# Shifting the activation tiles by half of 128 bytes against the weight tiles in SBUF

## The chip, the cores and the metric

The kernel runs on one core of a Trainium2 chip. The metric is the device time of one execution in microseconds: before the change the median of 3 runs is 2000.13 us (1999.19 to 2002.28).

## The reference, cut to what matters

Four blocks of a transformer-like model follow each other on one sequence of 256 positions with 2048 features, all in float32: an MLA attention layer (16 heads), a sliding-window attention layer (32 query heads, 4 key heads), a layer that holds MoBA attention (8 heads) beside a Mamba-2 mixer, and a feed-forward layer with a causal convolution of 3 taps.

```python
h = rmsnorm(x, layer_norm[i])
y, gate = mla_mixer(...) or swa_mixer(...)         # h @ w_in, then attention
x = x + (y * silu(gate)) @ w_out                   # twice, then rmsnorm
proj = h @ w_in_2                                  # q, k, v, z, xbc, dt
mixed = concat([attn, ssm]) @ w_out_2
u = causal_depthwise_conv(rms_norm(x) @ w_ffn_up)  # 2048 x 11264
f = (gelu(gate) * up) @ w_ffn_down                 # 5632 x 2048
```

Nearly all of the arithmetic is in these products of activations (256 rows) with weights.

## The kernel before, in words

**Three products for one.** Weights come from HBM in float32. The kernel multiplies in the type fp32r, in which an operand is rounded, and gets the accuracy back by splitting both operands into a rounded part ("high") and the rest ("low"): high x high + high x low + low x high are three matmuls into the same PSUM bank.

**Weight tiles.** SyncE loads 512 KB at a time into one of four slots `raw0..raw3` (`load`, 128 partitions x 1024 float32, 4096 bytes in each partition). ScalarE rounds it into `w_high0..3` (line 1025, `split`), VectorE writes the rest into `w_low0..3` (line 1458, `split`). Each of these engines works up to three tiles (`LEAD`) ahead of TensorE. A load into a slot waits until VectorE has made the low part of the tile that was there four tiles ago; ScalarE waits until TensorE has finished with the tile four back.

**Activations.** They lie transposed, with features on the partitions: `hT_high`, `hT_low` (the normalised input of a layer, 16 chunks of 256 positions, 1024 bytes a chunk), `cT_high`, `cT_low` (the MLA layer's two low-rank inputs), `yT_high`, `yT_low` (the gated output of an attention layer) and `hidden_high`, `hidden_low` (pieces of the feed-forward layer's hidden rows).

**Two kinds of product.** `block_b` (lines 450 to 452) loads 128 columns of a weight tile into the array and streams 256 columns of activations past it. `block_a` (lines 459 to 461) loads 128 columns of activations and streams 256 or 512 columns of weights past them; `down_step` (lines 1001 to 1003) does the same for the last layer with `hidden`. In a profile of this kernel the names behind `<-` don't say which of the two is streamed: at lines 450 to 452 it is the activations, at the others the weights. Each of these matmuls needs a weight load (LDWEIGHTS) of its own. Other products (attention scores, transposes, rotations) are in plain float32, at lines 486 and 489.

**Order of the work.** Each engine's stream is written out by hand, with semaphores between them. In the attention layers TensorE's stream alternates between projections and the attention of the group of heads before, so that the softmax on VectorE and ScalarE lies under matmuls.

**Where tensors lie.** `sb(name, shape)` places a tensor in SBUF behind the one that was asked for before it, in every partition at the same address, at the next multiple of 32 bytes. An `ExitStack` that is closed gives its room back, and the next tensor takes it. The first tensor of the program, `raw0`, starts at a multiple of 128 bytes. `raw`, `w_high`, `w_low`, `x`, `nx`, `hT_high` and `hT_low` are all multiples of 128 bytes long, so each of them starts at a multiple of 128. Counting the lengths on from there gives, as the remainder of the start address by 128:

| tensors | before | after the change |
|---|---|---|
| `raw`, `w_high`, `w_low` | 0 | 0 |
| `x`, `nx`, `hT_high`, `hT_low`, `constants` | 0 | 64 |
| `gain_rows`, `small` | 0 | 64 |
| `yT_high`, `yT_low`, `hidden_high`, `hidden_low` | 32 | 64 |
| `cT_high`, `cT_low`, `q_nope`, `k_nope` and others of the group `a1` | 96 | 64 |

All slices that the split products take start a multiple of 512 bytes into their tensor, so the table holds for every one of their operands.

Of the kernel before, what the change touches and what calls it, by code (L numbers as in the profile page):

```python
# [24 lines left out]
F32 = mybir.dt.float32  # L25
# [6 lines left out]
P = 128  # L32
# [144 lines left out]
def program(nc, a, out, toeplitz):  # L177
# [3 lines left out]
    def sb(name, shape, dt=F32, where=None):  # L181
        return (where or persistent).enter_context(nc.sbuf_tensor(name, shape, dt))
# [4 lines left out]
    with ctx:  # L187
        raw = [sb(f"raw{s}", [P, TILE]) for s in range(SLOTS)]
        whi = [sb(f"w_high{s}", [P, TILE], F32R) for s in range(SLOTS)]
        wlo = [sb(f"w_low{s}", [P, TILE], F32R) for s in range(SLOTS)]  # L190
        x = sb("x", [P, TT, D])
        nx = sb("nx", [P, TT, D])
        hTh = sb("hT_high", [P, DC, SEQ], F32R)
# [13 lines left out]
        xst = gbc[:, :].rearrange("p (t n) -> p t n", t=TT)  # L207
        small = sb("small", [P, 64])
        sq = sb("group_squares", [P, TT, 4])

        att = ExitStack()
        yTh = sb("yT_high", [P, DC, SEQ], F32R, att)
# [11 lines left out]
        rc = sb("row_rcp", [P, 2, 2], F32, att)  # L224

        a1 = ExitStack()
        cosm = sb("cos_mla", [P, SEQ], F32, a1)
        sinm = sb("sin_mla", [P, SEQ], F32, a1)
        coss = sb("cos_swa", [P, SEQ], F32, a1)
# [1962 lines left out]
```

How the kernel before makes its waits and increments, by code:

```python
def wait(eng, sem, count):  # L144
    if isinstance(count, int) and count <= 0:
        return
    eng.wait_ge(sem, count)
# [2 lines left out]
def after(eng, sem, count):  # L151
    eng.wait_ge(sem, count + 1)
# [15 lines left out]
    def done(self, ins):  # L169
        ins.then_inc(self.sem, 1)
        self.off += 1
        at = self.base + self.off
        self.eng.wait_ge(self.sem, at if not self.loop else at + self.i * self.loop)
# [190 lines left out]
        @block.sync  # L365
# [1 line left out]
            def load(tile, source, shape=(2, 512), i=0, n=0):  # L367
                s = tile % SLOTS
                if tile >= SLOTS:
                    sp.wait_ge(low_made, tile - SLOTS + 1 + i * n)
                c, w = shape
                sp.dma_start(raw[s][:, 0:c * w].rearrange("p (c n) -> p c n", c=c), source).then_inc(raw_loaded[s], 16)
# [50 lines left out]
            with sp.Fori(0, FC // 4) as i:  # L424
                for j in range(8):
                    load(T_DOWN + j, rows_of[:, bass.ds(i, 1), j % 4, j // 4, :], (1, TILE), i, 8)
            for b in (0, 1, 5, 2, 3, 6, 4, 7):
                mine = BY_POOL if b in BY_POOL else BY_DVE
                sp.wait_ge(ff["fin_pool" if b in BY_POOL else "fin"], mine.index(b) + 1)
                t, g = b // 4, b % 4
                sp.dma_start(out[t * P:(t + 1) * P, g * 512:(g + 1) * 512],
                             x[:, t, g * 512:(g + 1) * 512]).then_inc(stored, 16)
            sp.wait_ge(stored, 8 * 16)
# [7 lines left out]
            def ready(tile, i=0, n=0):  # L442
                pe.wait_ge(low_made, tile + 1 + i * n)
```

## Time and profile before

| | |
|---|---|
| median of the runs | 2000.13 us |
| the profiled execution | 2002.27 us |
| its span, first to last instruction | 2000.1 us |
| TensorE busy | 1907.7 us, 95% of the span, 13112 matmuls |
| TensorE weight loads busy | 1771.1 us, 89% |
| VectorE, ScalarE, GpSimd busy | 1110.5 us (56%), 896.9 us (45%), 151.3 us (8%) |
| mean granted TensorE clock | 0.982 of 2.4 GHz |
| read from HBM | 321.14 MB |

The profile lists one execution. A matmul's duration in it (`mean ns of one`) is longer than the time that it takes the array, because a matmul's way through the array overlaps with the next one's; what counts in a stream of matmuls is the distance from one start to the next.

### The profile page before, as it was taken

The numbers are of one execution on the slowest core, as the hardware profiler recorded it, in microseconds if no ns is written. First come the engines' busy times: TensorE is split into PE (matmuls) and PEld (weight loads), VectorE is DVE, ScalarE is ACT, GpSimd is POOL, SyncE is SP. The second block draws the span as 40 slices with busy tenths as digits, with TensorE's granted clock in tenths as the row PEclk, the third lists the DMA queues.
The fourth block names the chain that finished last, engine by engine and source line by source line (L and its number), as shares of the span: only waits on it lengthen the run. The fifth ranks groups of instructions, "written<-read, shape, count | busy, mean of one in ns | idle before, by whom it ended". The sixth has DMA issues, their size and how long they took to land.

```text
span 2000.1 us, 35228 instructions
## 1 busy us (share of the span) xinstructions
PE 1907.7 (95%) x13112; PEld 1771.1 (89%) x13112; DVE 1110.5 (56%) x1575; ACT 896.9 (45%) x1347; POOL 151.3 (8%) x177
## 2 busy tenths in 40 slices
PE   6899999889999997999999997999999999999997
PEld 5799998789999875999999786999999999988885
DVE  6555565545565655665555555556555556544444
ACT  5454444444444444454344444454444444433333
POOL 1001110000011000000000000100000000023322
PEclk9899999999999998999999998999999999999999
DMA  6455545535444454455554453555556555555553
GB/s 215 144 149 144 154 153 168 168 116 160 146 132 131 127 161 143 127 161 170 157 156 144 163 189 122 183 181 185 181 180 186 179 182 185 180 184 185 187 188 115
DMA packets 234781, 324.11 MB, mean 162 GB/s; under 512 B 12272, under 2 KB 170116, under 8 KB 234080
## 3 DMA queue, kind: packets, MB, share of 16 engines
q1 hardware_dynamic: 233296, 317.63, 51.0%
q0 software_dynamic: 1136, 4.58, 0.7%
q10 hardware_dynamic: 288, 1.09, 0.2%
q8 instruction: 39, 0.64, 0.1%
q14 instruction: 22, 0.18, 0.0%
HBM read 321.14 MB, written 2.11 MB: 162 GB/s over the span
## 4 chain that ended last, share of the span: by engine, by line
PE 92%; DVE 3%; ACT 2%; issue 1%; DMA 1%; POOL 0%; ACTq 0%; DVEq 0%; SPq 0%
PE bank L450 17%; PE bank L451 17%; PE bank L452 17%; PE bank L459 7%; PE bank L461 7%; PE bank L460 7%; PE bank L486 4%; PE bank L1002 3%; PE bank L1001 3%; PE bank L1003 3%; PE scores L486 3%; PE scores L1002 1%; PE scores L1001 1%; PE scores L1003 1%; PE bank L489 1%
## 5 line engine op out<-in xcount | busy, mean ns | idle before, releaser
L1458 DVE TENSOR_TENSOR w_low<-raw,w_high 128x1024 fp32r<-128x1024 f32 x603 | 739.3, 1229 | 756.2 <-ACT w_high L1025 755.7
L1025 ACT CAST w_high<-raw 128x1024 fp32r<-128x1024 f32 x603 | 630.2, 1048 | 828.9 <-PE bank L452 467.5
L450 PE MATMUL bank<-hT_high,w_high 128*128 128x256 f32 x2672 | 765.4, 286 | 8.8 <-issue 3.1
L451 PE MATMUL bank<-hT_low,w_high 128*128 128x256 f32 x2672 | 758.4, 284 | 0.0
L452 PE MATMUL bank<-hT_high,w_low 128*128 128x256 f32 x2672 | 758.4, 284 | 0.0
L450 PEld LDWEIGHTS bank<-hT_high,w_high 128*128 128x128 f32 x2672 | 515.4, 193 | 11.8 <-issue 11.4
L451 PEld LDWEIGHTS bank<-hT_low,w_high 128*128 128x128 f32 x2672 | 515.4, 193 | 1.1 <-issue 1.0
L452 PEld LDWEIGHTS bank<-hT_high,w_low 128*128 128x128 f32 x2672 | 515.2, 193 | 0.0
L459 PE MATMUL bank<-w_high,yT_high 128*128 128x512 f32 x384 | 152.9, 398 | 1.9 <-POOL yT_low L2076 1.9
L461 PE MATMUL bank<-w_high,yT_low 128*128 128x512 f32 x384 | 152.4, 397 | 0.0
L460 PE MATMUL bank<-w_low,yT_high 128*128 128x512 f32 x384 | 151.1, 394 | 0.0
L459 PE MATMUL bank<-w_high,hT_high 128*128 128x256 f32 (+1 forms) x352 | 107.6, 306 | 0.0
L460 PE MATMUL bank<-w_low,hT_high 128*128 128x256 f32 (+1 forms) x352 | 106.4, 302 | 0.0
L461 PE MATMUL bank<-w_high,hT_low 128*128 128x256 f32 (+1 forms) x352 | 106.3, 302 | 0.0
L1001 PE MATMUL bank<-w_high,hidden_high 128*128 128x512 f32 x264 | 104.1, 394 | 1.3 <-DVE up_conv L1994 1.3
L1002 PE MATMUL bank<-w_low,hidden_high 128*128 128x512 f32 x264 | 105.3, 399 | 0.0
L1003 PE MATMUL bank<-w_high,hidden_low 128*128 128x512 f32 x264 | 103.5, 392 | 0.0
L459 PEld LDWEIGHTS bank<-w_high,yT_high 128*128 128x128 f32 x384 | 72.1, 188 | 18.8 <-POOL yT_low L2076 1.6
L461 PEld LDWEIGHTS bank<-w_high,yT_low 128*128 128x128 f32 x384 | 72.1, 188 | 17.5
L460 PEld LDWEIGHTS bank<-w_low,yT_high 128*128 128x128 f32 x384 | 72.1, 188 | 17.4
L459 PEld LDWEIGHTS bank<-w_high,hT_high 128*128 128x128 f32 x352 | 67.2, 191 | 8.5 <-issue 6.1
L461 PEld LDWEIGHTS bank<-w_high,hT_low 128*128 128x128 f32 x352 | 67.2, 191 | 2.5
(270 smaller groups left out, 2022.6 us busy)
## 6 DMA issues: line engine op xcount, KB each, us to landing
raw<-in_w_up SPq DMA_DIRECT2D x176, 512.0 KB, 4.5
raw<-in_w_in SPq DMA_DIRECT2D x88, 512.0 KB, 3.5
raw<-in_w_down SPq DMA_DIRECT2D x88, 512.0 KB, 3.5
raw<-in_w_swa SPq DMA_DIRECT2D x72, 512.0 KB, 3.5
raw<-in_w_c SPq DMA_DIRECT2D x50, 512.0 KB, 3.8
raw<-in_w_mlao SPq DMA_DIRECT2D x32, 512.0 KB, 3.8
raw<-in_w_swao SPq DMA_DIRECT2D x32, 512.0 KB, 4.1
raw<-in_w_out SPq DMA_DIRECT2D x32, 512.0 KB, 3.6
```

The lines of the kernel that those rows point to most:

```text
L450: nc.tensor.matmul(to, h, act_h[:, chunk, :], start=first, stop=False, skip_group_check=True)
L451: nc.tensor.matmul(to, h, act_l[:, chunk, :], start=False, stop=False, skip_group_check=True)
L452: return nc.tensor.matmul(to, l, act_h[:, chunk, :], start=False, stop=last, skip_group_check=True)
L459: nc.tensor.matmul(to, ah, h, start=first, stop=False, skip_group_check=True)
L460: nc.tensor.matmul(to, ah, l, start=False, stop=False, skip_group_check=True)
L461: return nc.tensor.matmul(to, al, h, start=False, stop=last, skip_group_check=True)
L486: return nc.tensor.matmul(to, lhsT, rhs, start=start, stop=stop, skip_group_check=True)
L1001: nc.tensor.matmul(to, ah, whi[s][:, w], start=first, stop=False, skip_group_check=True)
L1002: nc.tensor.matmul(to, ah, wlo[s][:, w], start=False, stop=False, skip_group_check=True)
L1003: last = nc.tensor.matmul(to, al, whi[s][:, w], start=False, stop=True, skip_group_check=True)
L1025: nc.scalar.copy(whi[s][:, :], raw[s][:, :]).then_inc(high_made, 1)
L1458: v.tensor_tensor(wlo[s][:, :], raw[s][:, :], whi[s][:, :].bitcast(F32), ALU.subtract).then_inc(low_made, 1)
```

## The change

Three tensors that nothing reads or writes are put between the others. Their lengths are 64, 96 and 64 bytes in each partition.

```diff
         wlo = [sb(f"w_low{s}", [P, TILE], F32R) for s in range(SLOTS)]
+        sb("half_a_line_x", [P, 16])
         x = sb("x", [P, TT, D])
...
         sq = sb("group_squares", [P, TT, 4])
+        sb("half_a_line_y", [P, 24])
 
         att = ExitStack()
         yTh = sb("yT_high", [P, DC, SEQ], F32R, att)
...
         a1 = ExitStack()
+        sb("half_a_line_c", [P, 16], F32, a1)
         cosm = sb("cos_mla", [P, SEQ], F32, a1)
```

No instruction is added, removed or reordered; what changes is the start address of every tensor behind the first of the three, as in the table above.

## Rows read from the trace of the kernel before

**Rows 1.** The page, chain that ended last: shares of the span by engine.
```profile
PE 92%; DVE 3%; ACT 2%; issue 1%; DMA 1%; POOL 0%; ACTq 0%; DVEq 0%; SPq 0%
```
**Rows 2.** Windows: from:to, length, busy us (x instructions) by engine, TensorE clock, DMA share, GB/s.
```profile
0.00:25.00 25.00, 7.41 (x39) 6.95 (x40) 8.70 (x22) 15.07 (x24) 6.60 (x18) 1.00 0.76 263
25.00:75.00 50.00, 49.47 (x242) 41.74 (x240) 31.53 (x48) 24.27 (x36) 1.20 (x2) 1.00 0.58 171
1280.00:1730.00 450.00, 450.00 (x3752) 450.00 (x3752) 265.28 (x335) 209.04 (x252) 6.78 (x6) 1.00 0.59 182
```
**Rows 3.** TensorE's waits: who, total us, times, longest us.
```profile
PE bank L489 <- DVE prob L1507: 5.1, 5, 1.8
```
**Rows 4.** TensorE's groups by shape, first line of each three: name, shapes, count, busy us, mean ns.
```profile
L451 PE MATMUL bank<-hT_low,w_high 128*128 128x256 f32 x2672 | 758.4, 284 | 0.0
...
L459 PE MATMUL bank<-w_high,yT_high 128*128 128x512 f32 x384 | 152.9, 398 | 1.9 <-POOL yT_low L2076 1.9
...
L1001 PE MATMUL bank<-w_high,hidden_high 128*128 128x512 f32 x264 | 104.1, 394 | 1.3 <-DVE up_conv L1994 1.3
...
L459 PE MATMUL bank<-w_high,hT_high 128*128 128x256 f32 x288 | 82.6, 287 | 0.0
...
L450 PE MATMUL bank<-cT_high,w_high 128*128 128x256 f32 x160 | 46.0, 287 | 1.8 <-DVE cT_low L1473 1.8
...
L1001 PE MATMUL scores<-w_high,hidden_high 128*128 128x512 f32 x88 | 34.7, 394 | 0.0
...
L459 PE MATMUL bank<-w_high,hT_high 128*128 128x512 f32 x64 | 25.0, 391 | 0.0
...
L459 PE MATMUL bank<-w_high,cT_high 128*128 128x256 f32 x64 | 17.9, 280 | 0.0
```
**Rows 5.** Timeline, TensorE, feed-forward up: start us, duration us; first and seventh of seven.
```profile
1399.83 0.28 PE L450 MATMUL bank<-hT_high,w_high 128*128 128x256 f32 x1
...
1400.55 0.28 PE L450 MATMUL bank<-hT_high,w_high 128*128 128x256 f32 x1
```
**Rows 6.** The same view, first projection of the MLA layer; first and seventh of seven.
```profile
59.72 0.39 PE L459 MATMUL bank<-w_high,hT_high 128*128 128x512 f32 x1
...
61.08 0.39 PE L459 MATMUL bank<-w_high,hT_high 128*128 128x512 f32 x1
```
**Rows 7.** The same view, MLA output projection; first and seventh of seven.
```profile
299.69 0.39 PE L460 MATMUL bank<-w_low,yT_high 128*128 128x512 f32 x1
...
301.09 0.39 PE L460 MATMUL bank<-w_low,yT_high 128*128 128x512 f32 x1
```
**Rows 8.** The same view, feed-forward down; first and seventh of seven.
```profile
1799.78 0.39 PE L1003 MATMUL bank<-w_high,hidden_low 128*128 128x512 f32 x1
...
1801.18 0.39 PE L1003 MATMUL bank<-w_high,hidden_low 128*128 128x512 f32 x1
```
**Rows 9.** The same view, MLA projections from cT: 1st and 12th streamed; 1st loaded, 7th behind.
```profile
249.64 0.28 PE L451 MATMUL bank<-cT_low,w_high 128*128 128x256 f32 x1
...
250.96 0.28 PE L459 MATMUL bank<-w_high,cT_high 128*128 128x256 f32 x1
...
253.81 0.28 PE L459 MATMUL bank<-w_high,cT_high 128*128 128x256 f32 x1
...
254.51 0.28 PE L450 MATMUL bank<-cT_high,w_high 128*128 128x256 f32 x1
```
**Rows 10.** Groups of TensorE's weight loads: name, shapes, count, busy us, mean ns.
```profile
L451 PEld LDWEIGHTS bank<-hT_low,w_high 128*128 128x128 f32 x2672 | 515.4, 193 | 1.1 <-issue 1.0
...
L459 PEld LDWEIGHTS bank<-w_high,yT_high 128*128 128x128 f32 x384 | 72.1, 188 | 18.8 <-POOL yT_low L2076 1.6 <-issue 0.8
```
**Rows 11.** Groups of VectorE by shape: name, shapes, count, busy us, mean ns.
```profile
L1458 DVE TENSOR_TENSOR w_low<-raw,w_high 128x1024 fp32r<-128x1024 f32 x603 | 739.3, 1229 | 756.2 <-ACT w_high L1025 755.7
...
L1473 DVE SCALAR_TENSOR_TENSOR hT_low<-scores,column_vectors,hT_high 128x256 fp32r<-128x256 f32 x16 | 6.7, 477 | 0.0
...
L1473 DVE SCALAR_TENSOR_TENSOR cT_low<-bank,column_vectors,cT_high 128x256 fp32r<-128x256 f32 x8 | 3.3, 478 | 0.0
```

## The prediction

> **What bounds the kernel now.** I read the chain of waits first: TensorE is 92% of what ended last [rows 1]. Then a window of the longest stage, the feed-forward up product: TensorE busy for all of its 450 us, at a granted clock of 1.00 (2.4 GHz), VectorE for 265 and ScalarE for 209 us [rows 2]. TensorE's waits came third: the largest within an attention stage is 5.1 us in all [rows 3]. So the time is the number of matmuls times the distance between their starts. The groups by shape give the numbers, the timeline the distances.
>
> Counts [rows 4], each row standing for three lines of equal count. Activations hT, 256 columns streamed: 3 x (2672 + 288) = 8880. hT, 512 columns: 3 x 64 = 192. yT and hidden, 512 columns: 3 x (384 + 264 + 88) = 2208. cT: 3 x 160 = 480 with cT streamed and 3 x 64 = 192 with cT loaded.
>
> Distances, each from the starts of the first and the last of a few matmuls in a row, with the remainder by 128 of the activations' address in brackets (the weights' is 0):
> - hT (0), 256 columns: (1400.55 - 1399.83)/6 = 120.0 ns [rows 5]
> - hT (0), 512 columns: (61.08 - 59.72)/6 = 226.7 ns [rows 6]
> - yT (32), 512 columns: 1.40/6 = 233.3 ns [rows 7]
> - hidden (32), 512 columns: 1.40/6 = 233.3 ns [rows 8]
> - cT (96), 256 columns, cT streamed: 1.32/11 = 120.0 ns; cT loaded: 0.70/6 = 116.7 ns [rows 9]
>
> The first two differ by 106.7 ns for 256 columns, one column per 2.4 GHz cycle. Subtracting the columns (106.7 or 213.3 ns) leaves a fixed surcharge for each matmul: hT 13.3 ns, yT and hidden 20.0 ns, cT 13.3 ns streamed and 10.0 ns loaded. The surcharge is what an address can change, since yT and hT run the same instructions and differ by 6.7 ns. In these units of 6.7 ns (16 columns, 64 bytes of float32) it is two steps at remainder 0 and three at 32. The total is 9072 x 13.3 + 2208 x 20.0 + 480 x 13.3 + 192 x 10.0 = 121.0 + 44.2 + 6.4 + 1.9 = 173.5 us, and no more than that can go.
>
> **The change part by part.** No instruction comes or goes; only addresses move.
>
> *Operands of the split products.* The remainder becomes 64 for all activations. No row shows a split product there, so bounds: the surcharge gone, 0 ns, and the largest of the rows, 20.0 ns. Which way? Two readings of the rows. First, a matmul starts together with the weight load for the next one, and both read SBUF from their first column on. With hT both begin at remainder 0, and the load itself takes 193 ns, against 188 ns where yT is loaded [rows 10]: load and stream seem to hinder each other most when both begin at the same remainder. Second, of the two places that aren't a multiple of 64, loaded activations at 32 cost 20.0 ns and at 96, 64 bytes further, 10.0 ns (there in 256 columns taken from two places): so 64 bytes against the weights are worth up to 10 ns. Applied to remainder 0, the same shift takes 13.3 to 3.3 ns. I take 6.7 ns, one step instead of two: midway between nothing left and what hT has now, since cT streamed at 96 still pays 13.3 ns. The distances become 113.3 and 220.0 ns.
>
> The terms: hT 9072 x 6.7 = 60.5 us; yT and hidden 2208 x (20.0 - 6.7) = 29.4 us; cT 480 x 6.7 + 192 x 3.3 = 3.8 us. Sum 93.7 us, all on TensorE's path.
>
> *What could give it back.* The weight tile takes 24 matmuls, 2.88 us now and 2.72 us then. VectorE's step for it is 1.23 us [rows 11], and VectorE's share in the up stage goes from 265/450 = 59% to 62%. The loads go from 182 to 193 GB/s, and 263 GB/s was moved in the first 25 us [rows 2]. Neither becomes the bound. Where TensorE already waits for the softmax (5 times, 5.1 us [rows 3]), the output products that cover the wait get shorter and the chain under them doesn't: in front of each wait stand some 24 matmuls of 512 columns, 24 x 13.3 ns = 0.3 us, so 5 x 0.3 = 1.6 us come back there; with as much again at other edges, 3 us. If that cover were not there at all, the loss would still be only the saving made under it.
>
> *The other tensors.* VectorE, ScalarE and DMA also see moved tensors. One VectorE instruction stands in the trace at two remainders, hT_low (0) 477 ns and cT_low (96) 478 ns [rows 11], so I cost these at 0; 1 ns on each of 1575 VectorE instructions would be 1.6 us of busy time, and VectorE has 44% idle. The 1112 plain float32 matmuls keep their time; bounded by the 6.7 ns that 32 bytes were worth, that is 7.4 us either way, and I keep it for the range.
>
> Sum: the profiled execution took 2002.3 us; 2002.3 - 93.7 + 3 = 1911.6 us. The median lies 2.1 us below that execution, so 1909 us.
>
> **The rivals.**
>
> *Nothing is left of the surcharge.* If both hindrances are a meeting of load and stream in the same half of 128 bytes, 64 bytes apart they never meet. I leave 2 ns. Then 9072 x 11.3 + 2208 x 18.0 + 480 x 11.3 + 192 x 8.0 = 102.5 + 39.7 + 5.4 + 1.5 = 149 us, less 5 us for waits that appear: 1856 us. For it: the 193 ns loads. Against: cT streamed, 96 away, still pays 13.3 ns, and so would hT if part of the surcharge isn't a matter of address.
>
> *Only multiples of 64 count.* Remainder 32 costs one step more than 0 because 512 bytes from there touch one 64-byte piece more; 0 and 64 are alike. Then hT stays, yT and hidden save 2208 x 6.7 = 14.7 us, cT loaded loses 192 x 3.3 = 0.6 us: 1986 us. For it: the extra 6.7 ns is just one piece. Against: cT, off the multiples as well, pays no extra.
>
> *Slower: 64 is further off than 32.* The surcharge rises with the distance from the weights: 13.3 at 0, 20.0 at 32. The place is the start of every product of lines 450 to 461, the price one more step or more, 9072 x 6.7 = 60.5 us and 480 x 6.7 + 192 x 10.0 = 5.1 us for cT, yT unchanged: 2066 us. It decides as soon as hT's surcharge rises by more than 14.7 us / 9072 = 1.6 ns, what yT may save. It would be so if the load read its columns from the last to the first: then at equal remainders load and stream begin in different halves, and 64 bytes bring them together. For it: hT to yT, the cleanest pair of rows, goes this way. Against: cT at 96 pays less than yT, and hT's loads are the long ones.
>
> *Nothing happens.* The surcharge is in the instruction and 64 bytes do nothing: 2000 us. For it: 120.0 ns both at 0 and at 96 when activations are streamed. Against: the differences of up to 10 ns among the same lines.
> The Trainium skill, "TensorE: Matmul & The Clock Gate", section "Part 2: What happens when you issue a matmul", says that TensorE has two independent SBUF read ports, so that loading the next weights takes no bandwidth from the running matmul; by that rule this case is the right one. This trace doesn't bear it out in full: 193 against 188 ns for a load, and 233.3 against 226.7 ns for a matmul. The skill's "SBUF — State Buffer", section "Door 1: The DMA port swizzle", has 16-byte cachelines, by which 0, 32, 64 and 96 would all be alike; the same two rows speak against that.
>
> **How the numbers follow.** Forecast 0.36, no surcharge left 0.18, only multiples of 64 count 0.16, nothing happens 0.08, slower 0.22. A measurement of this kernel tells a difference from about 0.2% (4 us) on. Faster are the first three, 0.70; within 0.2% 0.08 and what falls between cases, 0.09; slower 0.21. The likeliest case's own range is 1890 to 1930 us (a third of a step either way is 30 us, the float32 matmuls within it). The range that I give, 1850 to 2004 us, holds the forecast, most of the case without surcharge, the 64-byte case and no change, about 0.78; it leaves out the slower case and a surcharge of exactly 0 (2000 - 168 = 1832 us).
>
> **What would show it.** Forecast right: in the up stage 113 ns from start to start, the weight loads there at 188 ns, the output projections and the down product at 220 ns, and all counts and VectorE's 1229 ns as they are. The case of the multiples of 64: 120.0 and 226.7 ns. Slower: 126.7 ns in the up stage with loads of 193 ns or more. My number is wrong if the surcharge isn't the same in long and short products, or if hT and yT, at the same remainder then, still differ.

## The result, and the profile after

The changed kernel takes 1979.06 us (median; 1976.92 to 1981.77) against 2001.2 us for the kernel before in the same comparison: a ratio of 0.988, 95% interval 0.987 to 0.990. That is 22 us faster, where 91 us were forecast. The profiled execution's span is 1977.4 us, 22.7 us shorter than before.

First the chain that ended last, then the windows, both of the changed kernel. They answer to [rows 1] and [rows 2].
```profile
PE 91%; DVE 4%; ACT 2%; issue 1%; DMA 1%; POOL 0%; DVEq 0%; SPq 0%; ACTq 0%
```
```profile
0.00:25.00 25.00, 7.56 (x42) 6.97 (x43) 9.33 (x23) 15.32 (x25) 6.57 (x18) 1.00 0.79 270
25.00:75.00 50.00, 49.78 (x238) 41.01 (x236) 30.90 (x46) 23.64 (x34) 1.20 (x2) 1.00 0.58 168
```
TensorE still bounds the kernel. The groups by shape, which answer to [rows 4] (the matmuls are 3 lines further down in the file than before):
```profile
L454 PE MATMUL bank<-hT_low,w_high 128*128 128x256 f32 x2672 | 748.6, 280 | 0.0
...
L462 PE MATMUL bank<-w_high,yT_high 128*128 128x512 f32 x384 | 153.2, 399 | 1.9 <-POOL yT_low L2079 1.9
...
L462 PE MATMUL bank<-w_high,hT_high 128*128 128x256 f32 x288 | 81.0, 281 | 0.0
...
L462 PE MATMUL bank<-w_high,hT_high 128*128 128x512 f32 x64 | 25.4, 397 | 0.0
```
The same counts; the groups with 256 columns have become shorter, the ones with 512 have not (hT's longer, 391 to 397 ns). Weight loads of streamed hT products answer to [rows 10]:
```profile
L454 PEld LDWEIGHTS bank<-hT_low,w_high 128*128 128x128 f32 x2672 | 505.5, 189 | 1.1 <-issue 1.0
```
They fell from 193 to 189 ns. VectorE's step for a weight tile is unchanged at 1229 ns, as in [rows 11]:
```profile
L1461 DVE TENSOR_TENSOR w_low<-raw,w_high 128x1024 fp32r<-128x1024 f32 x603 | 739.1, 1229 | 737.6 <-ACT w_high L1028 737.0
```

Now the distances between starts, in the timeline of the changed kernel (start us, duration us), two rows for each form of product, six products apart. They answer to [rows 6] to [rows 8]; the last pair is loaded hT with 256 columns streamed.
```profile
59.87 0.40 PE L462 MATMUL bank<-w_high,hT_high 128*128 128x512 f32 x1
...
61.27 0.40 PE L462 MATMUL bank<-w_high,hT_high 128*128 128x512 f32 x1
...
330.02 0.40 PE L463 MATMUL bank<-w_low,yT_high 128*128 128x512 f32 x1
...
331.42 0.40 PE L463 MATMUL bank<-w_low,yT_high 128*128 128x512 f32 x1
...
1800.00 0.40 PE L1005 MATMUL bank<-w_low,hidden_high 128*128 128x512 f32 x1
...
1801.40 0.40 PE L1005 MATMUL bank<-w_low,hidden_high 128*128 128x512 f32 x1
...
919.91 0.28 PE L462 MATMUL bank<-w_high,hT_high 128*128 128x256 f32 x1
...
920.59 0.28 PE L462 MATMUL bank<-w_high,hT_high 128*128 128x256 f32 x1
```
All products with 512 columns take 1.40/6 = 233.3 ns; hT's took 226.7 ns before, so they lost. Loaded hT with 256 columns takes 0.68/6 = 113.3 ns.

For the streamed products a long window is better than six products. The rows give TensorE's busy time and in brackets its matmuls, which include one or two that were already under way when the window began. First the kernel before, then the changed one; in each the MLA output projection (loaded yT, 512 columns), then the up stage (streamed hT, 256 columns).
```profile
320.00:370.00 50.00, 50.00 (x216) 40.22 (x215) 24.63 (x24) 21.35 (x26) 2.02 (x2) 1.00 0.57 181
1300.00:1600.00 300.00, 300.00 (x2503) 300.00 (x2502) 176.01 (x221) 140.15 (x170) 1.24 (x1) 1.00 0.59 182
```
```profile
320.00:370.00 50.00, 50.00 (x216) 40.30 (x215) 25.55 (x24) 21.06 (x26) 0.00 (x0) 1.00 0.58 185
1300.00:1600.00 300.00, 300.00 (x2549) 300.00 (x2548) 179.02 (x224) 142.07 (x173) 0.00 (x0) 1.00 0.60 185
```
216 and 216 in the first window: yT gained nothing. 2503 against 2549 in the second: 300/2549 = 117.7 ns instead of 119.9. The clock is 1.00 in all four.

The sum of it, with mean distances over the whole trace of one execution each (starts less than 150 ns apart, or 300 for 512 columns): streamed hT 8016 x (119.9 - 117.6) = 18.4 us; loaded hT, 256 columns, 864 x (119.9 - 114.4) = 4.8 us; loaded hT, 512 columns, 192 x (226.9 - 233.3) = -1.2 us; yT and hidden 0; cT 480 x 2.4 + 192 x 0.6 = 1.3 us. Together 23.3 us, for a span that is 22.7 us shorter.

### The profile page after: what moved, and what is told of

Read it like the earlier page. It is cut to its first block, busy times and chain, and to the rows that moved or that the text cites. A ratio compares the mean times of both kernels' runs of the same rounds, so it can differ in the third digit from the quotient of the medians.

```text
span 1977.4 us, 35228 instructions
## 1 busy us (share of the span) xinstructions
PE 1884.9 (95%) x13112; PEld 1747.2 (88%) x13112; DVE 1110.2 (56%) x1575; ACT 895.4 (45%) x1347; POOL 151.1 (8%) x177
## 4 chain that ended last, share of the span: by engine, by line
PE 91%; DVE 4%; ACT 2%; issue 1%; DMA 1%; POOL 0%; DVEq 0%; SPq 0%; ACTq 0%
PE bank L455 16%; PE bank L453 16%; PE bank L454 16%; PE bank L462 7%; PE bank L464 7%; PE bank L463 7%; PE bank L489 4%; PE bank L1004 3%; PE bank L1006 3%; PE bank L1005 3%; PE scores L489 3%; PE scores L1006 1%; PE scores L1004 1%; PE scores L1005 1%; PE bank L492 1%
## 5 line engine op out<-in xcount | busy, mean ns | idle before, releaser
L1461 DVE TENSOR_TENSOR w_low<-raw,w_high 128x1024 fp32r<-128x1024 f32 x603 | 739.1, 1229 | 737.6 <-ACT w_high L1028 737.0
L453 PE MATMUL bank<-hT_high,w_high 128*128 128x256 f32 x2672 | 756.0, 283 | 8.7 <-issue 3.1
L455 PE MATMUL bank<-hT_high,w_low 128*128 128x256 f32 x2672 | 750.3, 281 | 0.0
L454 PE MATMUL bank<-hT_low,w_high 128*128 128x256 f32 x2672 | 748.6, 280 | 0.0
L453 PEld LDWEIGHTS bank<-hT_high,w_high 128*128 128x128 f32 x2672 | 504.0, 189 | 12.1 <-issue 11.3
L454 PEld LDWEIGHTS bank<-hT_low,w_high 128*128 128x128 f32 x2672 | 505.5, 189 | 1.1 <-issue 1.0
L455 PEld LDWEIGHTS bank<-hT_high,w_low 128*128 128x128 f32 x2672 | 504.8, 189 | 0.0
L463 PEld LDWEIGHTS bank<-w_low,yT_high 128*128 128x128 f32 x384 | 72.2, 188 | 16.8
```

The costliest lines, as they stand in the source:

```text
L453: nc.tensor.matmul(to, h, act_h[:, chunk, :], start=first, stop=False, skip_group_check=True)
L454: nc.tensor.matmul(to, h, act_l[:, chunk, :], start=False, stop=False, skip_group_check=True)
L455: return nc.tensor.matmul(to, l, act_h[:, chunk, :], start=False, stop=last, skip_group_check=True)
L463: nc.tensor.matmul(to, ah, l, start=False, stop=False, skip_group_check=True)
L1461: v.tensor_tensor(wlo[s][:, :], raw[s][:, :], whi[s][:, :].bitcast(F32), ALU.subtract).then_inc(low_made, 1)
```

## The experiments

The kernels of this section move tiles, change what the split products read, or, in two of them, add short products or change an order. Their edits are given against the kernel before, unless said otherwise. Their main rows are the same two windows each time.

**All activations at 32, 96 or 0, weights at 0.** Three kernels, with other lengths of the fillers:
```diff
+        sb("pad_x", [P, 8])              # ahead of x: 8 (32 bytes), 24 (96), none (0)
...
+        sb("pad_y", [P, 24])             # ahead of the yT group
...
+        sb("pad_c", [P, 16], F32, a1)    # ahead of the cT group
```


> All activation tiles (hT, yT, hidden, cT) at remainder 32 by 128, weights at 0. Theory A (what counts is the distance of activation and weight tile by 128, for each form of product): loaded activations with 512 columns streamed 233.3 ns from start to start, as yT had at 32, now hT's first projection too (226.7 before); loaded activations with 256 streamed about 120; streamed activations 118 to 122. Total 2000 to 2015 us. Theory B (only multiples of 64 bytes are good places, 64 helped hT because both halves of a 128-byte line are used): streamed activations get worse than 120.0 ns at 32, 123 or more, total over 2025 us.

> All activation tiles at remainder 96, weights at 0. Theory A: 96 is 32 on the other side; no row shows 512 columns there, but loaded cT at 96 had 116.7 ns, so loaded activations cost 10 ns over their columns: 223 ns for 512 columns, 117 for 256; streamed 118 to 120. Total 1975 to 1990 us. Theory B: as at 32, over 2025 us.

> All activation tiles at remainder 0, weights at 0. Theory A: yT and hidden take 226.7 ns as hT did for 512 columns, 2208 x 6.7 = 14.7 us less than before; hT stays at 120.0 and 226.7: 1986 us. Rival (hT and yT differ by something else than the remainder, such as their distance in whole kilobytes or the stage): yT and hidden stay at 233.3 ns, 2001 us.

The windows at 32, at 96 and at 0:
```profile
320.00:370.00 50.00, 50.00 (x216) 40.23 (x216) 25.63 (x24) 21.35 (x26) 0.00 (x0) 1.00 0.60 185
1300.00:1600.00 300.00, 300.00 (x2574) 300.00 (x2573) 180.64 (x226) 143.51 (x175) 0.00 (x0) 1.00 0.61 188
```
```profile
320.00:370.00 50.00, 50.00 (x215) 40.17 (x215) 24.45 (x24) 21.29 (x26) 1.97 (x2) 1.00 0.58 180
1300.00:1600.00 300.00, 300.00 (x2503) 300.00 (x2502) 176.04 (x221) 140.23 (x170) 1.22 (x1) 1.00 0.59 182
```
```profile
320.00:370.00 50.00, 50.00 (x222) 41.39 (x222) 25.86 (x25) 21.37 (x26) 1.98 (x2) 1.00 0.61 187
1300.00:1600.00 300.00, 300.00 (x2502) 300.00 (x2501) 175.93 (x221) 140.08 (x170) 0.00 (x0) 1.00 0.59 182
```
At 32 the time is 1976.8 us (ratio 0.988, 0.986 to 0.989): the total that the change reached, at a place that isn't a multiple of 64. 2574 streamed products in 300 us are 116.6 ns each, better than at 64. Theory B, that only multiples of 64 are good, is out, and so is theory A's 2000 us: it had the loaded products with 512 columns right (233.3 ns) but expected nothing for the streamed ones. At 96 it is 2002.2 us (ratio 1.000, 0.999 to 1.001); both theories missed, A because 512 columns loaded cost 234.3 ns there and not the 223 ns that I had carried over from the 256 columns of cT. At 0 it is 1987.9 us (ratio 0.993, 0.991 to 0.995): 222 products instead of 216 in the first window, 226.7 ns, as theory A said. At place 0 hT, yT and hidden take the same, so here the place alone made their difference.

**Weights moved as well.** One filler of 64 bytes ahead of `raw0`, so that every tile moves and no distance changes.
```diff
+        sb("pad_w", [P, 16])
         raw = [sb(f"raw{s}", [P, TILE]) for s in range(SLOTS)]
```


> 64 bytes before raw0, so weights and activations all move by 64 bytes and their distances stay. Theory A (distance counts): every spacing as before the change, hT 120.0 and 226.7, yT and hidden 233.3 ns, 2001 us. Rival (the place of a tile itself counts, 64 is a better place than 0 for what is read): hT at 64 takes 118 ns, as after the change, 1980 us or less, since the weights are at 64 as well.

```profile
320.00:370.00 50.00, 50.00 (x216) 40.23 (x216) 24.98 (x23) 20.30 (x25) 2.73 (x2) 1.00 0.61 184
1300.00:1600.00 300.00, 300.00 (x2502) 300.00 (x2501) 175.99 (x221) 140.13 (x171) 0.76 (x1) 1.00 0.59 182
```
Both windows as before the change, and 2001.55 us (ratio 1.000, 0.999 to 1.001). hT lies at 64 here, as after the change, and gains nothing, because the weights lie at 64 too. What counts is the distance between the two operands; 64 bytes is the only common shift that was tried.

**What the surcharge is made of: one operand that doesn't walk.** Four kernels with the tiles where they were before the change.
```diff
-                h, l = cols(wh), cols(wl)
+                h, l = (cols(w)[:, 0:1].to_broadcast([P, P]) for w in (wh, wl))     # load one column
...
-                nc.tensor.matmul(to, h, act_h[:, chunk, :], ...
+                nc.tensor.matmul(to, h, act_h[:, chunk, 0:1].to_broadcast([P, SEQ]), ...   # stream one column
...
+                h, l, to = cols(wh)[:, 0:64], cols(wl)[:, 0:64], to[0:64]           # load 64 columns
```


> Tiles where they were before the change. In the products with streamed activations (lines 450 to 452) the weight load reads the first of its 128 columns 128 times, so it touches one place of SBUF instead of 512 bytes; this leaves out 127 of 128 weight columns. Theory A (the surcharge is what load and stream do to each other when they read SBUF): hT streamed falls from 120.0 ns to 107 to 113. Theory C (the surcharge belongs to the instruction, with the stream's own address alone behind its size): 120.0 ns stays.

> Tiles where they were before the change. In the products with streamed activations the stream reads the first of its 256 columns 256 times; this leaves out the other activation columns. Theory A: the stream touches one place only, the load still walks over 512 bytes: less surcharge, 107 to 115 ns. Theory C: 120.0 ns if the surcharge belongs to the instruction, about 107 if the stream's own walk makes it; then e5_load_one_column must show no fall.

> Tiles where they were before the change. The weight load of the products with streamed activations takes 64 columns (256 bytes) instead of 128; this leaves out half of the output rows of these products. Theory A: half as many meetings, a surcharge of 6.7 instead of 13.3 ns, 113.3 ns from start to start. Theory C: 120.0 ns stays. If the load's own length set the pace, it would fall below 106.7 ns at no point, since the stream is still 256 columns.

> Tiles as before the change. In the products with streamed activations load and stream both read one column over and over, so neither walks through SBUF; this leaves out the other columns. If the surcharge is made by the two walks (8.4 ns gone without the stream's, 4.3 without the load's): 107 to 110 ns. If a part belongs to the instruction: it stays at the 111.6 ns of e5b_stream_one_column.

The up stage with one column loaded, one column streamed, and both:
```profile
1300.00:1600.00 300.00, 300.00 (x2574) 300.00 (x2573) 180.00 (x225) 143.98 (x176) 0.00 (x0) 1.00 0.61 187
```
```profile
1300.00:1600.00 300.00, 300.00 (x2689) 300.00 (x2689) 189.24 (x239) 148.59 (x182) 0.00 (x0) 1.00 0.64 196
```
```profile
1300.00:1600.00 300.00, 300.00 (x2689) 300.00 (x2688) 189.41 (x238) 148.45 (x183) 0.00 (x0) 1.00 0.65 196
```
Over the whole trace, streamed hT takes 119.9 ns as it is, 115.7 with one column loaded, 111.7 with one column streamed, and 111.7 with both. The 115.7 is a mean of several lasting values: stretches at 113.3 to 114.2, others (the whole up stage among them) at 116.7, and a few at 120.0 ns. With a standing stream there is one value alone, 111.6 to 112.4 ns in every piece of up to 48 products in a row. So of the surcharge of 13.2 ns, 5.0 ns stay when nothing walks and 8.2 ns need the stream's walk; letting the load alone stand still takes away 3.3 ns in the up stage and 4.2 ns in the mean. Once the stream stands still, it makes no difference what the load reads. That fits neither theory in full: reading matters, as A says, but 5.0 ns stay. That no address could remove these is not shown, since the standing operands were tried at one place only. The rival in which 2 ns are left would need 109 ns, and no form in any run came below 111.4.

Loading 64 columns gave something that nobody expected. The rows are a window of the sliding-window layer's projections and one of the up stage, in the same execution:
```profile
435.00:455.00 20.00, 20.00 (x179) 20.00 (x178) 8.58 (x7) 9.39 (x10) 0.00 (x0) 1.00 0.68 186
1300.00:1600.00 300.00, 300.00 (x2502) 300.00 (x2501) 175.95 (x221) 140.35 (x170) 0.00 (x0) 1.00 0.59 182
```
The same product, at the same places by 128 bytes, takes 113.3 ns or up to 1 ns more in nearly all runs of products up to 1060 us, as A had it, and 120.0 ns in every one from 1206 us on, through the whole up stage, as C had it. The load of 64 columns takes 135 ns instead of 193 (mean), so its length doesn't set the pace of the up stage. A theory that gives each distance by 128 bytes one duration can't have this. I read it as a rhythm, in which one load and stream hinder the next and more than one rhythm can last; that is an interpretation, and what is shown is that more than one pace lasts.

Each of these four kernels ran once: 1972.2 us with one column loaded, 1938.2 with one streamed, 1976.3 with 64 loaded, 1936.2 with both operands standing.

**The same for 512 columns.** The stream's weights as one column, in the products with loaded activations.
```diff
-                            nc.tensor.matmul(to, ah, whi[s][:, w], ...
+                            nc.tensor.matmul(to, ah, whi[s][:, 0:1].to_broadcast([P, 512]), ...
```


> Tiles as before the change. In the products with loaded activations (lines 459 to 461 and 1001 to 1003) the stream reads one weight column over and over; this leaves out the other weight columns. If the same thing makes the surcharge there: yT and hidden fall from 233.3 ns to 216 to 219, hT's first projection from 226.7 to the same, so that remainder 32 and 0 no longer differ. Rival (for loaded activations the load's own walk at 32 makes the extra step): yT and hidden stay some 7 ns above hT.

```profile
320.00:370.00 50.00, 50.00 (x233) 43.70 (x232) 27.50 (x26) 23.57 (x31) 0.00 (x0) 1.00 0.65 202
```
233 products instead of 216, and 1954.5 us (one run). Over the trace hT's first projection (loaded, at 0) takes 216.5 ns instead of 226.9, hidden (at 32) 216.5 instead of 233.3, yT (at 32) 217.5 instead of 233.4. The whole difference between the places goes when the stream stands still; 3.2 ns over the columns remain (4.2 in yT's mean). The rival, that a load at 32 costs more by itself, is out.

**Places between.** Every tensor aligned to 16 bytes instead of 32, with fillers such that all activations lie at 16, 48 or 80 (`pad_x` of 4, 12 or 20 elements; one of 4 elements ahead of `raw0` moves weights and activations alike).
```diff
-        return (where or persistent).enter_context(nc.sbuf_tensor(name, shape, dt))
+        return (where or persistent).enter_context(nc.sbuf_tensor(name, shape, dt, align_bytes=16))
```


> All activation tiles at remainder 16, weights at 0. If what counts is how many 64-byte pieces an operand touches: 16 is like 32 for the loaded ones (233.3 ns at 512 columns). If it is the distance itself: between 0 and 32, 226.7 to 233.3 ns loaded, 116.8 to 120 streamed.

> All activation tiles at remainder 48. By pieces: as 32, 233.3 ns loaded at 512 columns, 116.8 streamed. By distance: between 32 and 64, 116.8 to 117.7 ns streamed, 113.3 to 118.3 loaded with 256 columns, 233.3 loaded with 512.

> All activation tiles at remainder 80. By pieces: as 96, 234.3 ns loaded at 512 columns and 119.9 streamed. By distance: between 64 and 96, 117.7 to 119.9 ns streamed, 113.3 to 117.5 loaded with 256 columns.

They took 1988.3, 1980.3 and 1997.4 us (one run each). With the runs above, the mean distances in ns by the activations' place, each from one execution:

| place | 0 | 16 | 32 | 48 | 64 | 80 | 96 |
|---|---|---|---|---|---|---|---|
| streamed hT, 256 columns | 119.9 | 117.8 | 116.8 | 118.3 | 117.6 | 119.6 | 119.9 |
| loaded hT, 256 columns | 119.8 | 118.3 | 118.3 | 119.3 | 114.4 | 118.8 | 117.5 |
| loaded hidden, 512 columns | 226.7 | 233.3 | 233.3 | 230.0 | 233.3 | 231.9 | 234.3 |

Neither the count of 64-byte pieces nor a value between the neighbours describes it: 16 is like 32 for 512 columns, as the pieces say, but 48 is 3.3 ns better than either neighbour, and 64 stands out for one form only. The forms don't share a best place.

Two things in these traces speak against reading the table as a law. Its streamed row holds means of several lasting paces at 16 (113.3, 116.7 and 118.7 ns), 32 (116.7 and 117.8) and 80 (118.3 and 119.9). And at 48 the loaded products with 512 columns don't agree with each other: hT's first projection, then yT's output projection, six products apart.
```profile
59.76 0.40 PE L463 MATMUL bank<-w_high,hT_high 128*128 128x512 f32 x1
...
61.16 0.40 PE L463 MATMUL bank<-w_high,hT_high 128*128 128x512 f32 x1
...
329.72 0.40 PE L463 MATMUL bank<-w_high,yT_high 128*128 128x512 f32 x1
...
331.11 0.39 PE L463 MATMUL bank<-w_high,yT_high 128*128 128x512 f32 x1
```
Over the trace hT's take 233.3 ns, yT's and hidden's 230.1 and 230.0, all at remainder 48 by 128. Counted by 256 bytes, hT lies 48 and the other two 176 bytes from the weights. At 32 the same difference does nothing (hidden takes 233.3 ns both 160 bytes off, before the change, and 32 bytes off, with everything at 32). Whether the distance matters beyond 128 bytes at some places, or this is one more pair of paces, was not tested.

**Is the pace a rhythm that can be chosen?** In the changed kernel itself, two timelines of the same products in the Mamba-2 part, six products apart:
```profile
946.53 0.28 PE L453 MATMUL bank<-hT_high,w_high 128*128 128x256 f32 x1
...
947.24 0.28 PE L453 MATMUL bank<-hT_high,w_high 128*128 128x256 f32 x1
...
953.46 0.28 PE L453 MATMUL bank<-hT_high,w_high 128*128 128x256 f32 x1
...
954.14 0.28 PE L453 MATMUL bank<-hT_high,w_high 128*128 128x256 f32 x1
```
0.71/6 = 118 ns in one run of 48 products and 0.68/6 = 113.3 ns, my forecast, in the next. Of 179 pieces of up to 48 products each, 7 keep 113.3 ns; 172 keep 117.8.

That the addresses don't decide it can be seen in one loop. In the kernel with hT at 64 and yT at 0 (the last experiment below) the third piece of a turn of the Mamba-2 loop runs the same instructions at the same addresses in each of its three turns. Here are the first and the second turn, twelve products apart:
```profile
939.04 0.28 PE L452 MATMUL bank<-hT_high,w_high 128*128 128x256 f32 x1
...
940.40 0.28 PE L452 MATMUL bank<-hT_high,w_high 128*128 128x256 f32 x1
...
993.07 0.28 PE L452 MATMUL bank<-hT_high,w_high 128*128 128x256 f32 x1
...
994.48 0.28 PE L452 MATMUL bank<-hT_high,w_high 128*128 128x256 f32 x1
```
1.36/12 = 113.3 ns and 1.41/12 = 117.5 ns; over the whole pieces 113.3 and 117.8, and 113.3 again in the third turn.

Two kernels try to move the up stage into the faster one, both in the layout after the change. One puts a short product ahead of each half group, the other changes the order of the three.
```diff
+                        k = (32, 64, 96, 112)[2 * u + half]
+                        nc.tensor.matmul(to[:, 0:k], hTh[:, 0, 0:P], hTl[:, 0, 0:k], start=True, stop=True, ...)
```
```diff
-                nc.tensor.matmul(to, h, act_l[:, chunk, :], start=False, stop=False, ...)
-                return nc.tensor.matmul(to, l, act_h[:, chunk, :], start=False, stop=last, ...)
+                nc.tensor.matmul(to, l, act_h[:, chunk, :], start=False, stop=False, ...)
+                return nc.tensor.matmul(to, h, act_l[:, chunk, :], start=False, stop=last, ...)
```


> The layout after the change, with one short product more (32, 64, 96 or 112 columns streamed, 4 widths in turn) ahead of each of the 88 half groups of 48 products of the feed-forward up stage; its result is overwritten. After the change the whole stage kept 117.8 ns, while 7 of 180 runs of the same products in other stages kept 113.3 ns. Theory D (the pace is a rhythm of load and stream that is taken up at the start of an unbroken run and then kept): some of the 88 half groups, always behind the same width, keep 113.3 ns and the others 117.8. Rival (117.8 ns is what this distance costs in this stage): all stay at 117.8 ns. The 88 added products cost about 88 x 60 ns = 5 us by their columns.

> The layout after the change; in the products with streamed activations the three matmuls come as high x high, low weights x high activations, high weights x low activations, so the same operand is streamed twice in a row instead of loaded twice in a row. If the sequence of the three decides which pace a run takes up at distance 64: streamed hT leaves 117.8 ns, 113.3 or 120.0 in most runs of products, total 1955 to 1962 or 1990 us and more. If only the addresses count: 117.8 ns and 1979 us.

The up stage has 44 half groups of 96 products, not the 88 of 48 that the expectation counted. Two of the added products in the timeline:
```profile
1409.91 0.19 PE L983 MATMUL bank<-hT_low,hT_high 128*128 128x64 f32 x1
...
1421.32 0.21 PE L983 MATMUL bank<-hT_low,hT_high 128*128 128x96 f32 x1
```
11.41 us lie between them; 96 products of 117.8 ns are 11.31. All 43 half groups behind the first (which runs partly at half clock) are back at 117.8 ns within ten products, whatever the width, and the kernel takes 1982.9 us (one run). So theory D's forecast missed and its rival's came true. The test was a weak one, though: the short product and the first one behind it take 228 to 230 ns together at every width, so the four widths hardly changed when a half group started. The other order gives 117.6 ns, 11 of 179 pieces at 113.3 ns instead of 7, and 1978.56 us (ratio 0.987, 0.986 to 0.989), level with the change. So in this stage 117.8 ns is what the products return to; what lets a few pieces elsewhere keep 113.3 ns was not found, and that the pace is a rhythm stays an interpretation.

**The best places together.**
```diff
+        sb("pad_x", [P, 8])              # hT and cT at 32;  the other kernel: 16, hT and cT at 64
+        sb("pad_y", [P, 16])             # yT and hidden at 0;                  8
+        sb("pad_c", [P, 24], F32, a1)    # cT;                                  none
```


> The best place of each form by the runs so far: hT and cT at remainder 32 (116.8 ns streamed), yT and hidden at 0 (226.7 ns loaded, 512 columns). If each product's pace depends on its own two operands alone, the savings add up: 8016 x 3.2 + 864 x 1.6 - 192 x 6.6 + 2208 x 6.6 = 25.7 + 1.4 - 1.3 + 14.6 = 40.4 us, 2001 - 40 = 1961 us. Rival: part of it is lost at waits that TensorE then meets in the attention stages, 1968 us or more.

> hT and cT at remainder 64 as after the change, yT and hidden at 0 as in e3_acts_at_0. If each form keeps the spacing of its own distance: streamed hT 117.7, loaded hT with 256 columns 113.5 to 114.4, with 512 columns 233.3, yT and hidden 226.7 ns; 1979 - 14.7 = 1964 us, level with e7_hT32_yT0. Rival: yT's 233.3 ns after the change came from something that the whole layout did, and the saving is under 5 us.

```profile
320.00:370.00 50.00, 50.00 (x222) 41.42 (x221) 25.70 (x25) 21.95 (x27) 0.00 (x0) 1.00 0.60 189
1300.00:1600.00 300.00, 300.00 (x2549) 300.00 (x2548) 180.19 (x228) 142.96 (x175) 0.00 (x0) 1.00 0.60 186
```
```profile
320.00:370.00 50.00, 50.00 (x222) 41.39 (x221) 26.35 (x25) 22.39 (x30) 0.00 (x0) 1.00 0.61 192
1300.00:1600.00 300.00, 300.00 (x2549) 300.00 (x2548) 178.68 (x225) 142.87 (x175) 0.00 (x0) 1.00 0.60 186
```
1964.92 us (ratio 0.983, 0.980 to 0.985) with hT at 32 and 1964.77 us (ratio 0.980, 0.979 to 0.982) with hT at 64: both beat the change, by 14 us in the medians and by 12 and 16 us in the ratios, by leaving yT and hidden at 0. The second is what its expectation said, form by form (117.7, 114.4, 233.3 and 226.7 ns). The first lies between its forecast of 1961 us and its rival's 1968. With hT at 32 the up stage has 2549 products in the window and had 2574 in the kernel with everything at 32, though hT lies in the same place in both: 117.8 against 116.7 ns. That is a second pair of lasting paces at one distance, worth 1.1 x 4224 = 4.6 us in this stage, about what the forecast missed by. The other tensors' places need not be behind it: the kernel with everything at 32 has both, 116.7 ns in most pieces and 117.8 in others of the same execution. It may be behind the wide spread of this kernel's runs (1958.5 to 1975.0 us); that isn't shown.

## Why the prediction was wrong

**What bounds the kernel: right.** TensorE's starts were the path and stayed it. The counts left out 48 streamed hT products that write to `scores` (16 at each of three lines, 0.1 us of the saving) and were right otherwise, and a table of counts and distances gives the saving to within 1 us.

**The direction and the reading of yT against hT: right, but the direction stood on two readings that don't carry it.** The surcharge depends on the distance between the two operands (64 bytes before everything change nothing), and at 0 hT and yT take the same. The first reading took loads of 193 against 188 ns as the mark of a hindrance at equal remainders. These are the loads of yT with yT at 0, and the loads of the streamed hT products where neither operand walks:
```profile
L461 PEld LDWEIGHTS bank<-w_high,yT_high 128*128 128x128 f32 x384 | 72.1, 188 | 17.0 <-POOL yT_low L2078 1.6 <-issue 0.8
...
L451 PEld LDWEIGHTS bank<-hT_low,w_high 128*128 128x128 f32 x2672 | 515.6, 193 | 1.1 <-issue 1.0
```
At remainder 0 yT's loads still take 188 ns, and with the shortest way from start to start, 111.7 ns, the others still take 193. So the length of a load doesn't tell how much the products hinder each other. The second reading is taken up below.

**The step that failed: one surcharge of 6.7 ns for every product at remainder 64.** I put cases of three forms in one list (streamed 256, loaded 256, loaded 512 columns) and carried what one showed to the others.
- Streamed hT, forecast 60.5 us with the rest of hT, kept 10.9 ns: 8016 x 2.3 = 18.4 us. Forecast for these alone were 53.4 us, so they are nine tenths of the error in hT's term, and 35 of the 70 us by which the sum of 93.7 us was too high.
- Loaded hT with 256 columns went to 113.3 ns where it runs undisturbed, just as forecast, but these are 864 products (mean 114.4 ns, 4.8 us saved).
- Loaded yT and hidden, forecast 29.4 us, gave 0: 64 is no better than 32 for 512 columns. hT's 192 such products lost 6.4 ns each, a loss that the forecast had no term for.
The midpoint between 0 and 13.3 ns had no row at the new distance under it, and the second reading joined cT's 256 columns to yT's 512 to make a shift of 64 bytes worth 10 ns. The runs show that this pair doesn't measure a shift: at 96 with 512 columns it is 234.3 ns, no better than at 32. The prediction had named the sign itself: its number is wrong if long and short products don't have the same surcharge. Why the forms differ stays open.

**The lower bound was too low.** I took the columns alone as the floor. 5.0 ns remain with both operands standing still (256 columns), 3.2 ns with the stream standing still (512), and 111.7 ns is the least that hT's products reached in any run.

**The rivals.** "Only multiples of 64 count" named the nearest time, 1986 us, for the wrong reason: it had yT gaining and hT not, and the reverse happened, so that its time lay near is luck. "Nothing is left" fell with the floor. "Slower" was right for 192 products. "Nothing happens" fell with the 22 us. The Trainium skill's page "TensorE: Matmul & The Clock Gate", section "Part 2: What happens when you issue a matmul", says that loading the next weights takes no SBUF read bandwidth from the running matmul. That what a load reads costs the matmuls nothing doesn't hold for these fp32r products: in the up stage one takes 119.9 ns beside a load that walks and 116.6 ns beside one that doesn't.

**What gives back: small, but not put to the test.** 23.3 us by distances and 22.7 us in the span leave 0.6 us, against 3. The waits for the softmax, which had been 5.1 us, are
```profile
PE bank L492 <- DVE prob L1510: 5.2, 5, 1.8
```
The products got shorter by a quarter of what was forecast, and those with 512 columns, which cover these waits, not at all. So the 3 us could not show.

**The range** of 1850 to 2004 us held the time; the likeliest case's own range of 1890 to 1930 us did not. It allowed for a third of a step more or less in every product at once, not for one form that gains while another gains nothing.

## What to carry to other kernels

In a stream of fp32r matmuls with a fresh weight load each, the distance in SBUF between the loaded and the streamed operand, taken by 128 bytes, is worth here, in means of one execution each, 3.1 ns (streamed, 256 columns), 5.4 ns (loaded, 256) and 7.6 ns (loaded, 512) a product between the best and the worst place, which is 3 to 5%. Measure the start-to-start distance for each form (which operand is loaded, how many columns are streamed) at each place, and place each tile by its own form: here loaded tiles with 512 columns streamed at the weights' own remainder, and the streamed tile 32 or 64 bytes off, which together saved 35 to 39 us of 2000. Between 32 and 64 the runs don't decide. Don't carry a place from one form to another, and don't take the columns alone as the floor.

## What the runs showed of the hardware that had not been expected

- The pace of a product isn't fixed by its operands' places. The same instructions at the same addresses kept 113.3 ns in two turns of a loop and 117.8 in the turn between them. At the same places by 128 bytes, products kept 113.3 or 120.0 ns (64 columns loaded), 113.3 or 117.8 ns (distance 64) and 116.7 or 117.8 ns (distance 32), over pieces of 48 products up to the whole up stage of 4224.
- When the stream reads one column again and again, 8.2 ns of 119.9 ns go, and 16.8 ns of 233.3, with as many columns streamed, and the lasting paces of streamed hT come down to one.
- A 16-byte shift matters: loaded with 512 columns, 226.7 ns at 0 and 233.3 ns at 16.
